# Stage borders of a two-block transformer kernel: GpSimd tables later, a square sum on ScalarE, roots with a bias, the norm in four pieces, chunks bank by bank

## The reference

```
x = x + 0.5 * swiglu(rms_norm(x, ffn1_norm))          # ffn1, d_ff 2816
h = rms_norm(x, mix_norm); proj = h @ w_in            # the mixer
x = x + concat(dilated_attention, hgrn2) @ w_out
x = x + 0.5 * swiglu(rms_norm(x, ffn2_norm))          # ffn2
# layer 0: state space (s5) and pooling mixers; layer 1: stick-breaking attention
x = layer_norm(alpha * x + mixer(x)); x = layer_norm(alpha * x + moe(x) + ple(x))

rms_norm(x)   = x * rsqrt(mean(x*x) + 1e-6) * w
layer_norm(x) = (x - mean) * rsqrt(var + 1e-5) * g + b
```

## Time and profile before

| | us |
|---|---|
| median of 3 runs | 1241.16 (1240.19 to 1241.46) |
| the profiled execution, own time | 1240.4 |
| its span, first to last instruction | 1238.5 |
| PE busy | 1196.8 (97%) |
| DVE busy | 645.9 (52%) |
| ACT busy | 509.6 (41%) |
| GpSimd busy | 206.2 (17%) |

### The profile page before, as it was taken

The page is one execution under the profiler, slowest core; times in us unless marked ns, Lnnn a source line. Parts: engine busy times, 40 slices in busy tenths (PEclk is TensorE's granted clock), DMA queues, the critical chain, the costliest instruction groups (busy, mean ns, idle before and its releaser), DMA issues.

```text
span 1238.5 us, 16766 instructions
## 1 busy us (share of the span) xinstructions
PE 1196.8 (97%) x6900; PEld 843.6 (68%) x6900; DVE 645.9 (52%) x943; ACT 509.6 (41%) x750; POOL 206.2 (17%) x207
## 2 busy tenths in 40 slices
PE   6999999999999999999999999998999999999995
PEld 5888888887688888888884444334898884444432
DVE  7666557756777787649772111104677771111103
ACT  5655555647465455514441111114587542111112
POOL 0000000240399994002000000000033200000000
PEclk9999999999999999989999999999999999999998
DMA  9555554551545555425788999999635688999996
GB/s 391 203 202 176 198 189 151 187 187 69 177 172 188 187 200 178 167 111 195 303 320 368 427 426 426 427 427 420 216 111 204 268 325 358 427 426 427 427 427 236
DMA packets 49617, 338.23 MB, mean 273 GB/s; under 512 B 5504, under 2 KB 5504, under 8 KB 11008
## 3 DMA queue, kind: packets, MB, share of 16 engines
q1 hardware_dynamic: 47808, 330.54, 68.2%
q10 hardware_dynamic: 1728, 6.55, 1.6%
HBM read 336.02 MB, written 1.05 MB: 272 GB/s over the span
## 4 chain that ended last, share of the span: by engine, by line
PE 82%; DVE 8%; DMA 5%; ACT 3%; issue 1%; SPq 0%; POOL 0%; DVEq 0%; ACTq 0%
PE pb L180 81%; DMA extra<-in_moe_w 4%; DVE halves L341 1%; ACT halves L333 1%; DMA ring<-in_ffn_w 1%; DVE XTb L447 1%; DVE XN L389 0%; DVE XTb L441 0%; DVE XN L400 0%; PE pb L2256 0%; DVE Xs L457 0%; SPq L372 0%; ACT Xs L1711 0%; DVE SM L1628 0%; DVE decayed L1531 0%
## 5 line engine op out<-in xcount | busy, mean ns | idle before, releaser
L180 PE MATMUL pb<-XTb,halves 128*128 128x256 f32 (+1 forms) x2080 | 332.5, 320 | 4.6 <-DVE XTb L447 3.5
L341 DVE TENSOR_TENSOR halves<-ring,halves 128x2048 fp32r<-128x2048 f32 (+1 forms) x120 | 280.1, 2355 | 91.1 <-ACT halves L333 91.1
L180 PEld LDWEIGHTS pb<-XTb,halves 128*128 128x128 f32 x2080 | 299.5, 190 | 39.3 <-issue 3.1
L333 ACT CAST halves<-ring 128x2048 fp32r<-128x2048 f32 (+1 forms) x122 | 226.9, 1875 | 47.6 <-PE pb L180 44.6
L180 PE MATMUL pb<-halves,XTb 128*128 128x512 f32 x768 | 180.7, 394 | 3.0 <-DVE XTb L1751 1.8
L180 PEld LDWEIGHTS pb<-halves,XTb 128*128 128x128 f32 x768 | 143.4, 189 | 34.4 <-DVE halves L341 1.6
L180 PE MATMUL pb<-ring,gather 128*64 128x512 f32 x672 | 152.1, 595 | 0.0
L2396 DVE TENSOR_TENSOR slots_h<-slots_silu,pb 128x256 f32<-128x256 f32 x32 | 13.5, 422 | 243.5 <-ACT slots_silu L2355 243.5
L180 PE MATMUL pb<-halves,HTh 128*128 128x512 f32 x352 | 109.1, 391 | 0.0
L180 PEld LDWEIGHTS pb<-ring,gather 128*64 128x64 f32 x672 | 46.3, 137 | 87.0 <-issue 87.0
L180 PE MATMUL pb<-extra,gather 128*64 128x512 f32 x336 | 80.0, 596 | 0.0
(11 more groups left out here) (374 smaller groups left out, 1387.6 us busy)
## 6 DMA issues: line engine op xcount, KB each, us to landing
ring<-in_moe_w SPq DMA_DIRECT2D x120, 1024.0 KB, 15.4
ring<-in_ffn_w SPq DMA_DIRECT2D x66, 1024.0 KB, 4.8
extra<-in_moe_w SPq DMA_DIRECT2D x62, 1024.0 KB, 13.5
ring<-in_w_tok SPq DMA_DIRECT2D x10, 1024.0 KB, 4.8
ring<-in_ple_gate SPq DMA_DIRECT2D x8, 1024.0 KB, 4.7
extra<-in_moe_w SPq DMA_DIRECT2D x16, 512.0 KB, 21.4
ring<-in_w_out SPq DMA_DIRECT2D x4, 1024.0 KB, 4.7
ring<-in_ab_out SPq DMA_DIRECT2D x4, 1024.0 KB, 4.8
```

The source lines that it names most:

```text
L180: return e.matmul(out, l, r, start=start, stop=stop, **kw)
L333: e.copy(split_of(n)[0], raw_of(n)).then_inc(*high.mark(n))
L341: e.tensor_tensor(l, raw_of(n), h.bitcast(F32), ALU.subtract).then_inc(*low.mark(n))
```

## The change

It has six parts.

- Roots with a bias. In the RMS norms the small instruction that adds and scales the two square sums goes; the root reads one sum as input and the other as its bias, and the norm product multiplies by 32, the root of 1024, as its second scalar. In the LayerNorms the instruction that adds 1e-5 goes; the root reads the variance and a bias tile holding 1e-5 (`eps_n`, set by a memset in `dve_ssm`).
- At the mixer and ffn2 borders ACT takes the square sum of the third quarter, (1, 0), with its accumulator; the weight cast between the two roots goes, so that the next `act_split` call, behind the chunks, does two blocks.
- The norm product of the second half is made in four pieces of 256 columns; PE waits for each piece on its own.
- The eight chunks go in the order 0, 2, 1, 3, 4, 6, 5, 7. DVE starts a chunk when ACT has written that one; ACT starts an odd chunk only when DVE is through with the even one of its bank. PE takes the chunks in that order in `pe_ffn` and `pe_proj`, waiting for each.
- ffn1's chunks use banks 6, 7, 2, 3 in place of 4 to 7.
- `pool_tables` also waits for the last low part of ffn2's chunks.

```diff
 def dve_rms(e, c, key, add, shared):
...
                     add(t, h)
+                    if shared and t and h == 0:
+                        continue
...
-                i.then_inc(*c.chain.mark())
-                e.wait_ge(*c.chain.now())
-                e.tensor_scalar(r, ss[:, 2 * t:2 * t + 1], ss[:, 2 * t + 1:2 * t + 2], 1.0 / D, ALU.add,
-                                ALU.mult).then_inc(*mean_sq.mark(key, t))
+                i.then_inc(*squares.mark(key, t))
                 e.wait_ge(*root.at(key, t))
                 e.reciprocal(r, r).then_inc(*c.chain.mark())
                 e.wait_ge(*c.chain.now())
...
+                pieces = 4 if t else 2
+                n = D // pieces
+                for q in range(pieces):
+                    f = slice(q * n, q * n + n)
+                    e.tensor_scalar(XN3[:, t, f], X3[:, t, f], r, ROOT_D, ALU.mult, ALU.mult).then_inc(*xn.mark(key, t, q * 4 // pieces))
...
+        def act_root(e, key, shared=None):
             for t in range(2):
+                if t and shared:
+                    e.wait_ge(*x_new.at(shared, 1, 0))
+                    e.activation(XN3[:, 1, 0:512], X3[:, 1, 0:512], ACT.Square, accum_out=ss[:, 2:3]).then_inc(*act_squares.mark(key))
+                    e.wait_ge(*act_squares.now())
                 r = rs[:, t:t + 1]
-                e.wait_ge(*mean_sq.at(key, t))
-                e.activation(r, r, ACT.Sqrt).then_inc(*root.mark(key, t))
-                if t == 0 and between:
-                    between()
+                e.wait_ge(*squares.at(key, t))
+                e.activation(r, ss[:, 2 * t:2 * t + 1], ACT.Sqrt, bias=ss[:, 2 * t + 1:2 * t + 2]).then_inc(*root.mark(key, t))
...
         def act_xt(e, key, weight, into=(4, 5, 6, 7)):
+            if weight is not None:
+                for i in BANK_BY_BANK:
+                    e.wait_ge(*turned.at(key, i // 2))
+                    if i % 2:
+                        e.wait_ge(*xt_low.at(key, i - 1))
+                    e.activation(XT3[0][:, i, :], banks[into[i // 2]][:, i % 2 * 256:i % 2 * 256 + 256], ACT.Copy,
+                                 scale=weight[:, i:i + 1]).then_inc(*xt_high.mark(key, i))
+                return
...
         def dve_xt(e, key, weight, into=(4, 5, 6, 7)):
+            if weight is not None:
+                for i in BANK_BY_BANK:
+                    e.wait_ge(*xt_high.at(key, i))
+                    e.scalar_tensor_tensor(XT3[1][:, i, :], banks[into[i // 2]][:, i % 2 * 256:i % 2 * 256 + 256], weight[:, i:i + 1],
+                                           XT3[0][:, i, :].bitcast(F32), ALU.mult, ALU.subtract).then_inc(*xt_low.mark(key, i))
+                return
...
@@ pe_ffn, and pe_proj alike
-                    for k in range(8):
-                        if n == 0 and half == 0 and k % 2 == 0:
-                            e.wait_ge(*xt_low.at(f.key, k // 2))
+                    for k in BANK_BY_BANK:
+                        if n == 0 and half == 0:
+                            e.wait_ge(*xt_low.at(f.key, k))
...
@@ pool_tables
             e.wait_ge(*s5_f.at())
             e.wait_ge(l_cm, 16)
+            e.wait_ge(*xt_low.at("ffn2", 7))
...
@@ dve_ssm
+            e.memset(eps_n, 1e-5).then_inc(*c.chain.mark())
+            e.wait_ge(*c.chain.now())
...
@@ act_norm and act_hat
-                e.activation(r, r, ACT.Sqrt).then_inc(*deviation.mark(i, t))
+                e.activation(r, mv2[:, t, 1:2], ACT.Sqrt, bias=eps_n).then_inc(*deviation.mark(i, t))
...
@@ dve_norm, and dve_hat alike
-                then(e.bn_aggr(m, st4[:, t, :, :]))
-                e.tensor_scalar(r, m[:, 1:2], 1e-5, None, ALU.add).then_inc(*variance.mark(i, t))
+                e.bn_aggr(m, st4[:, t, :, :]).then_inc(*variance.mark(i, t))
+                e.wait_ge(*variance.now())
...
@@ act_program
-            act_root(e, "mix", lambda: act_split(e, c, ffns[0].last + 3))
+            act_root(e, "mix", "ffn1")
...
-            act_root(e, "ffn2", lambda: act_split(e, c, index["w_out", 3] + 3))
+            act_root(e, "ffn2", "mix")
```

More of the change, by code:

```diff
@@ L379, in build, with dve_rms @@
         rs, ss = small(2), small(4)
-        mean_sq, root, xn = signal("mean_sq"), signal("root"), signal("xn")
+        squares, act_squares, root, xn = signal("squares"), signal("act_squares"), signal("root"), signal("xn")
+        ROOT_D = 32.0
+        BANK_BY_BANK = (0, 2, 1, 3, 4, 6, 5, 7)
+        assert ROOT_D * ROOT_D == D
         turned, xt_high, xt_low, x_new = signal("turned"), signal("xt_high"), signal("xt_low"), signal("x_new")
-        def dve_rms(e, c, key, add):
+        def dve_rms(e, c, key, add, shared):
             for t in range(2):
@@ L426, in act_xt @@
                 e.wait_ge(*turned.at(key, kp))
[L427 to L433, removed]
@@ L436, in dve_xt @@
             for kp in range(4):
                 P = banks[into[kp]]
[L438 to L449, removed]
+                k = slice(2 * kp, 2 * kp + 2)
@@ L451, in build @@
+                e.wait_ge(*xt_high.at(key, kp))
+                e.tensor_tensor(XT3[1][:, k, :], P.rearrange("p (k t) -> p k t", k=2), XT3[0][:, k, :].bitcast(F32),
+                                ALU.subtract).then_inc(*xt_low.mark(key, 2 * kp))
+                xt_low.value[key, 2 * kp + 1] = xt_low.n
         acc_half, acc_part = signal("acc_half"), signal("acc_part")
@@ L606, in pe_proj @@
             for c in range(2):
-                for k in range(8):
-                    if fresh and c == 0 and k % 2 == 0:
-                        e.wait_ge(*xt_low.at(fresh, k // 2))
+                for k in BANK_BY_BANK:
+                    if fresh and c == 0:
+                        e.wait_ge(*xt_low.at(fresh, k))
                     i = mm3(e, P[:, c * 256:c * 256 + 256], both(W, lambda x: x[:, k, c * 128:c * 128 + 128]),
@@ L620, in pe_tok @@
                     for k in range(begun if half == 0 and t == 0 else 0, 4):
-                        if fresh and t == 0 and k % 2 == 0:
-                            e.wait_ge(*xt_low.at(fresh, 2 * half + k // 2))
+                        if fresh and t == 0:
+                            e.wait_ge(*xt_low.at(fresh, 4 * half + k))
                         i = mm3(e, banks[b][:, :], both(XT3, lambda x: x[:, 4 * half + k, t * 128:t * 128 + 128]),
@@ L1597, in build @@
         GB = XN
-        bst, mv, rstd = small(24), small(4), small(2)
+        bst, mv, rstd, eps_n = small(24), small(4), small(2), small(1)
         st4 = bst.rearrange("p (t h s) -> p t h s", t=2, h=2)
@@ L1680, in dve_hat @@
                 then(e.bn_stats(st4[:, t, 1, :], banks[2 * t + 1][:, :]))
-                then(e.bn_aggr(mv2[:, t, :], st4[:, t, :, :]))
-                e.tensor_scalar(r, mv2[:, t, 1:2], 1e-5, None, ALU.add).then_inc(*variance.mark(2 * i + 1, t))
+                e.bn_aggr(mv2[:, t, :], st4[:, t, :, :]).then_inc(*variance.mark(2 * i + 1, t))
                 e.wait_ge(*deviation.at(2 * i + 1, t))
@@ L1708, in act_hat @@
                     e.wait_ge(*variance.at(2 * i + 1, t))
-                    e.activation(r, r, ACT.Sqrt).then_inc(*deviation.mark(2 * i + 1, t))
+                    e.activation(r, mv2[:, t, 1:2], ACT.Sqrt, bias=eps_n).then_inc(*deviation.mark(2 * i + 1, t))
                 e.wait_ge(*shifted.at(i, t))
@@ L2594, in pe_program @@
             e.wait_ge(l_con, 16)
[L2595 to L2596 removed]
+            pe_turn(e, "ffn1", XN3, lambda t, q: xn.at("ffn1", t, q), None, (6, 7, 2, 3), fine=True)
+            idle(2, banks[0])
             pe_ffn(e, ffns[0])
[L2598 removed]
+            pe_turn(e, "mix", XN3, lambda t, q: xn.at("mix", t, q), lambda: idle(2, banks[0]), fine=True)
             pe_mix(e)
[L2600 removed]
+            pe_turn(e, "ffn2", XN3, lambda t, q: xn.at("ffn2", t, q), lambda: idle(2, banks[0]), (6, 7, 2, 3), fine=True)
             pe_ffn(e, ffns[1])
@@ L2676, in dve_program @@
             dve_split(e, c, ffns[0].last + 2)
-            dve_rms(e, c, "mix", add("ffn1", "ffn1", ffns[0].last, None, 0.5))
+            dve_rms(e, c, "mix", add("ffn1", "ffn1", ffns[0].last, None, 0.5), True)
             dve_xt(e, "mix", par("nm"))
@@ L2681, in dve_program @@
             dve_split(e, c, index["w_out", 3] + 2)
-            dve_rms(e, c, "ffn2", add("mix", "w_out", index["w_out", 3], None, 1.0, 2))
+            dve_rms(e, c, "ffn2", add("mix", "w_out", index["w_out", 3], None, 1.0, 2), True)
             dve_xt(e, "ffn2", par("n2"), (6, 7, 2, 3))
```

27 lines of the change are left out of this document (12 added, 15 removed).

## The result

The changed kernel takes 1249.55 us (median of 4 runs, 1249.43 to 1250.98), the kernel before 1241.31 us on the same chip (4 runs, 1240.19 to 1242.83). The medians lie 8.2 us apart; the ratio on record is 1.0060, interval 1.0048 to 1.0072 (the two medians alone give 1.0066). So the changed kernel is slower, clear of noise. The prediction was 1240.8 with a range of 1238.0 to 1242.8 and 0.13 for slower by over 0.2%. It was wrong, in direction and in size. The profiled execution took 1250.98 us for a span of 1249.2, 1.4 us more than the median; the one before took 1240.4 for 1238.5. The two traces thus differ by 10.7 us, 2.5 more than the medians.

The account below looks back on a forecast made before the run. TensorE (PE), busy 97% of the span, was taken as the bound. The terms 1.0 + 0.7 + 0.14 - 1.06 - 0.22 - 0.2 gave 0.36 us gained off 1241.16: 1240.8, range 1238.0 to 1242.8.

Parts of the forecast that it names:

- the moved cast: Both borders: weight cast goes behind the chunks, GpSimd's tables start 11 us later under ffn2; all put at nothing.
- Rival C: Late ACT and DVE starve PE at the start and at ffn2's fourth block: 2.0 us lost, 1243.2; chance 0.14.
- B: Rival at both borders: DVE's time is PE's time, 4.8 us gained, 1236.4, with half of it 1238.6; chance 0.24.
- The start: First FFN: chunk order delays ACT's casts and DVE's splits, PE waits for two sums; loss 1.06 us.
- Mixer border: Border into the mixer: earlier norm product and chunks bank by bank gain 1.0 us, bounds 0.2 and 1.8.
- ffn2 border: Border into ffn2: without GpSimd beside it, DVE's chain is shorter; gain 0.7 us, bounds 0 and 1.6.
- State space projection: Chunks come in pairs but the order takes chunk 2 second, so PE waits: loss 0.22 us, bounds 0 and 0.6.
- LayerNorm roots: Removed TENSOR_SCALAR gains 0.14 us before the first MoE; the root's pointer loses 0.2 after it.
- Square and Sqrt in one set: ACT's Squares and roots at the borders share one table set, so no added table load; otherwise some 0.3 late per border.

Follow-up runs that it names:

- e2: The kernel before with only the wait of GpSimd's tables for ffn2's last low part added: 1248.55 us, ratio 1.0048.
- e3: The changed kernel, its wait of the tables kept, with DVE's two lam steps one group later in ffn2: 1244.09 us, ratio 1.0010.
- e1: The changed kernel without the one wait that holds GpSimd's tables back: 1247.48 us, ratio 1.0036 to the kernel before.
- e4: e1 with the first FFN's chunks in the old order and handshake: 1245.99 us, ratio 1.0028 to the kernel before.
- e5: e4 with GpSimd pausing after its sixth operation until the last norm product, and holding its widest turns until DVE's second lam group is done: 1242.14 us, 0.9997.
- e9: e5 with GpSimd's pause after its third operation in place of its sixth: 1242.38 us, ratio 1.0000 to the kernel before.
- e6: e4 with GpSimd pausing after its sixth operation until the last norm product, without waiting for DVE's lam operations: 1246.24 us, ratio 1.0036.
- e10: e8 with GpSimd also waiting for DVE's second lam group ahead of its widest turns: 1241.33 us, ratio 0.9988 to the kernel before.
- e8: e4 with the ffn2 border, its chunks and the first FFN's norm pieces in their old form: 1241.81 us, ratio 0.9999 to the kernel before.

## Why the prediction was wrong

- **The failing step** is in the moved cast: "GpSimd's tables start 11 us later, under ffn2. They ended over 40 us before the next use of GpSimd, so their end is at nothing". The end was indeed free, but the step put the move at nothing by its end alone, not by what the same operations meet on the way. Between ffn2's fifth block and its last pair the changed kernel's trace loses 7.7 us (5.4 of waits for sums, 1.5 of clock behind the longest). e2 shows that this one line alone brings 5.6 there (366.02 to 504.49), and e3 that all of it goes when the lam operations move away; the other 2.1 come only with the rest of the change, and no run separates them. The tables' wide operations were moved onto a group of DVE's (`dve_lam`) that no sentence of the prediction names.
- **Rival C** had the engine pair, the price of a subtraction (3.39) and the direction, at 0.14, with 1243.2. It put the collision at the fourth block with the long subtractions, 1.3 us. No wait came there: DVE's sum there was done at 354.35, against the 354.6 allowed. The short operations pay more in all, since each of the seven loses 0.7 to 1.1 us, as a subtraction does. (Under B, half of the gain gives 1238.8 and not 1238.6; nothing hangs on it.)
- **The start** was right in place and shape: ACT's next cast at 18.05 less 0.55 of later DMA is 17.50 (said 17.37), the wait at the fifth block 0.56 (said 0.57). The sum was 1.06, measured 1.43: up to the fifth block 0.54 was lost beside the wait, in place of 0.3, and behind it, to the mixer border, 0.33 in place of 0.19.
- **Mixer border**: said 1.0, measured 0.83 (132.62 us from its transposes to those of ffn2, after 131.79). **ffn2 border**: said 0.7, measured 0.50 (34.39 us to the fifth block, after 33.89), and only because GpSimd was held back; e1 and e4 lose 1.2 and 1.05 there. That the gain hangs on the wait of the tables stood in the prediction ("without GpSimd beside it"), but the two were summed as if they were independent.
- **State space projection**: said -0.22, measured -0.18. The first matmul comes as before (2.81 and 2.82 us behind the transposes), and the loss lies in the first loop over the chunks, as said: the first 16 matmuls take 2.32 us in place of 2.14, and the first 96 take 11.76 to the next row in place of 11.58. **LayerNorm roots**: said +0.14 and -0.2. The second transposes of the norm before the MoE wait 0.73 in place of 0.86, a gain of 0.13; after the first MoE 0.16 is lost (854.36 to 861.49, now 864.13 to 871.42).
- **Square and Sqrt in one set**: right. ACT's Square of the mixer border takes 0.63, and no table load lies between it and the root at 203.05. After the first MoE the root starts 0.01 us behind its table load (the load ends at 855.58, the root starts at 855.59; kernel before); in the mixer's loop it comes 1.65 us behind, since it waits for DVE.
- The terms other than the tables sum to -0.3 as measured (0.83 + 0.50 + 0.13 - 0.16 - 1.43 - 0.18 = -0.31), against +0.36 said. Each lies within 0.4 us of its forecast; that part was sound, but for the sign of its sum.

## What to carry to other kernels

Before a block of GpSimd work is moved, list what DVE does in the new window as closely as in the old, the shortest instructions first: here each lost 0.7 to 1.1 us beside GpSimd operations of 1.2 to 1.7, and the place to look is where a DVE result frees a buffer that PE wants. Hold GpSimd with a wait at the two or three spots where DVE is critical and not with one wait ahead of everything: that took the loss away here (e5), though it made nothing clearly faster. And look at the reserve of the engine that PE will wait for: in e9 PE came 1.5 us early to a sum with 1.0 us of reserve, and kept nothing of it.

## What the runs showed of the hardware

- Beside GpSimd's 128x512 operations the short DVE instructions slowed most for their length: TENSOR_SCALAR 128x512 from 0.43 to 1.16 us (once 1.37), TENSOR_TENSOR from 0.68 to 1.54 and 1.78, the weight subtraction only from 2.29 to 2.98 and 3.38. One input or two made no great difference to the loss: the TENSOR_SCALAR reads one tensor only and lost 0.73 us (once 0.94), those with two inputs lost 0.74 to 1.10.
- Two stands of PE were followed by a loss beyond their own time. After 3.57 us (changed kernel) and 3.32 us (e6) the granted clock fell to 0.50 for about 3 us (in e6 from 1 us into the block), and the 64 matmuls behind it took 1.5 and 1.6 us more. After waits of 1.53 (changed kernel), 1.61 (e1) and 2.12 us (e2) it stayed at 1.00.
- About 2 us of the two profiled executions' difference lies in TensorE's clock in later stages. Windows of the kernel before, then of the changed one, from the same matmul of the state space stage and from the same one after the first MoE (the windows are not equally long):

```profile
542.70:553.00 10.30, 10.30 (x189) 9.53 (x190) 4.41 (x9) 1.16 (x2) 1.01 (x1) 0.67 0.01 3
...
861.50:870.00 8.50, 8.12 (x35) 6.42 (x36) 7.66 (x13) 7.66 (x11) 0.00 (x0) 1.00 0.94 346
```

```profile
551.40:561.00 9.60, 9.58 (x174) 9.25 (x178) 2.71 (x6) 0.00 (x0) 0.00 (x0) 0.50 0.01 3
...
871.40:880.00 8.60, 8.58 (x31) 6.96 (x32) 7.53 (x13) 7.52 (x11) 0.00 (x0) 0.80 0.94 343
```

  The granted clock is 0.67 over the first stretch of the kernel before and 0.50 over that of the changed one; over the second it is 1.00 and 0.80. In both kernels PE had just stood for 1.6 us before the first stretch. In the changed kernel PE takes 9.91 us in place of 8.63 from there to the same matmul (551.42 to 561.33, before 542.66 to 551.29), of which 1.1 is left at the stage's end, and 23.47 in place of 22.51 after the MoE (871.42 to 894.89, before 861.49 to 884.00). Whether the change brings this is not shown, with one profile of each kernel. The state space stretch has the clock of the kernel before in e10 alone (0.64 over 9.6 us; 0.50 to 0.52 in the other versions), the stretch after the MoE its length in e3 alone (22.48; 23.3 to 24.2 in the others).
- The mean granted clock and the time of single runs go together in part. In the runs beside e8 the kernel before took 1244.1 us at a mean granted clock of 0.989 (5 runs), 1242.1 at 0.991 (10) and 1241.6 at 0.992 (8); e8 took 1242.9 (2), 1241.2 (3) and 1241.0 (2), 0.6 to 1.2 less at equal clock, near the 0.83 of its border. e10 does not follow this: 1241.6 at 0.990 (2), 1241.4 at 0.991 (5), 1241.5 at 0.992 (4). Comparing at equal clock may help with effects under 1 us; these runs do not prove it.
